# Row gathers and gate scatters in turn on GpSimd's queue, in a decoder step with product-key experts

## The reference

```
def peer_chunk(h, w_q, sub_keys, u_tab, v_tab):
    q = (h @ w_q).reshape(C, PEER_HEADS, 2, D_KEY // 2)
    s = jnp.einsum('cphd,phkd->cphk', q, sub_keys).astype(jnp.float32)
    s1, i1 = lax.top_k(s[:, :, 0], PEER_TOPK)
    s2, i2 = lax.top_k(s[:, :, 1], PEER_TOPK)
    ...
    top_s, top_i = lax.top_k(cand, PEER_TOPK)
    e = jnp.take_along_axis(cidx, top_i, axis=-1)
    g = jax.nn.softmax(top_s, axis=-1)
    a = jax.nn.gelu(jnp.einsum('cpkd,cd->cpk', u_tab[e], h)).astype(jnp.float32)
    return jnp.einsum('cpk,cpkd->cd', (g * a).astype(v_tab.dtype), v_tab[e])
```

## Time and profile before

| | us |
|---|---|
| median of 3 runs | 1051.7 |
| lowest and highest | 1051.29, 1053.26 |
| the profiled execution, its own time | 1053.38 |
| its span (first to last instruction) | 1051.7 |
| TensorE busy | 1023.4 |
| VectorE busy | 806.2 |
| ScalarE busy | 534.9 |
| GpSimd busy | 360.9 |

### The profile page before, as it was taken

One profiled execution on the slowest core, in us unless ns is written; L12 is line 12 of the kernel. 1 busy time (PEld: TensorE's weight loads), 2 busy tenths in 40 slices (PEclk: granted clock), 3 DMA queues, 4 the chain that ended last, 5 costly groups with the idle time before them and its releaser, 6 DMA issues.

```text
span 1051.7 us, 22444 instructions
## 1 busy us (share of the span) xinstructions
PE 1023.4 (97%) x6977; PEld 919.5 (87%) x6977; DVE 806.2 (77%) x1778; ACT 534.9 (51%) x995; POOL 360.9 (34%) x288
## 2 busy tenths in 40 slices
PE   7999999999999999999999999999999999999997
PEld 7997746999999998999999999988878888888875
DVE  4334276686889997895677589979888888888888
ACT  5435565454545444444344645555555555555553
POOL 0244500000057778878888781011011010100100
PEclk9999997999999999999999999999999999999999
DMA  7655997343478879999999967878888888888872
GB/s 271 261 212 171 351 296 233 120 153 129 169 212 232 233 207 273 309 246 273 342 347 358 294 172 237 318 276 296 301 305 296 287 286 294 282 297 284 290 262 96
DMA packets 132346, 270.05 MB, mean 257 GB/s; under 512 B 30112, under 2 KB 79296, under 8 KB 130480
## 3 DMA queue, kind: packets, MB, share of 16 engines
q1 hardware_dynamic: 98352, 205.23, 57.3%
q0 software_dynamic: 33952, 64.33, 21.7%
HBM read 240.99 MB, written 30.57 MB: 258 GB/s over the span
## 4 chain that ended last, share of the span: by engine, by line
PE 41%; POOL 15%; DMA 7%; issue 5%; DVE 3%; ACT 1%; SPq 0%; DVEq 0%; ACTq 0%; POOLq 0%
POOL gates L548 14%; PE ps L1094 10%; PE ps L1095 10%; PE ps L1096 10%; DMA activations<-u_out 4%; PE ps L1071 3%; PE ps L604 3%; PE ps L605 3%; PE ps L606 3%; POOL urow L556 1%; DMA gates<-spread_out,spread_at 1%; DMA a_in<-activations 1%; DVE w_lo L1501 1%; DMA urow<-in_u_rows_dram,expert 1%; DVE w_lo_last L1501 0%
## 5 line engine op out<-in xcount | busy, mean ns | idle before, releaser
L1501 DVE TENSOR_TENSOR w_lo<-ring,w_hi 128x512 fp32r<-128x512 f32 (+1 forms) x439 | 386.3, 885 | 119.2 <-ACT w_hi L1151 100.0
L1151 ACT CAST w_hi<-ring 128x512 fp32r<-128x512 f32 (+1 forms) x437 | 338.0, 774 | 77.9 <-PE ps L1096 58.2
L604 PE MATMUL ps<-h_hi,w_hi 128*128 128x256 f32 (+1 forms) x1128 | 325.1, 288 | 6.7 <-DVE w_lo L1501 4.8
L605 PE MATMUL ps<-h_lo,w_hi 128*128 128x256 f32 (+1 forms) x1128 | 321.6, 285 | 0.0
L606 PE MATMUL ps<-h_hi,w_lo 128*128 128x256 f32 (+1 forms) x1128 | 319.8, 283 | 0.0
L548 POOL DMA_INDIRECT gates<-spread_out,spread_at x128 | 229.7, 1795 | 134.8 <-DVE spread_out L1934 82.5
L604 PEld LDWEIGHTS ps<-h_hi,w_hi 128*128 128x128 f32 x1128 | 215.3, 191 | 8.9 <-DVE w_lo L1501 4.6
L605 PEld LDWEIGHTS ps<-h_lo,w_hi 128*128 128x128 f32 x1128 | 214.5, 190 | 0.0
L606 PEld LDWEIGHTS ps<-h_hi,w_lo 128*128 128x128 f32 x1128 | 212.6, 188 | 0.0
L1094 PE MATMUL ps<-w_hi,y_hi 128*128 128x512 f32 x496 | 193.9, 391 | 0.8 <-DVE y_lo L2026 0.5
L1096 PE MATMUL ps<-w_lo,y_hi 128*128 128x512 f32 x496 | 193.0, 389 | 0.0
(11 more groups left out here) (385 smaller groups left out, 1251.6 us busy)
## 6 DMA issues: line engine op xcount, KB each, us to landing
ring<-in_uT_dram SPq DMA_DIRECT2D x128, 512.0 KB
ring<-in_v_dram SPq DMA_DIRECT2D x128, 512.0 KB
activations<-u_out SPq DMA_DIRECT2D x128, 128.0 KB
a_in<-activations SPq DMA_DIRECT2D x124, 128.0 KB, 4.6
ring<-in_w_in_dram SPq DMA_DIRECT2D x22, 512.0 KB
gates<-spread_out SPq DMA_DIRECT2D x8, 1024.0 KB, 9.6
ring<-in_w_q_dram SPq DMA_DIRECT2D x16, 512.0 KB
gates<-gates POOLq DMA_DIRECT2D x8, 1024.0 KB, 6.9
```

Source lines behind the costliest of these rows:

```text
L604: mm(out, hi, hi_, start=start, stop=False)
L605: mm(out, hi, lo_, start=False, stop=False)
L1151: nc.scalar.copy(w_hi[slot][:, x], ring[:, ring_slot, x]).then_inc(part_hi, 2 if half is None else 1)
L1501: V.tensor_tensor(w_lo[slot][:, x], ring[:, ring_slot, x], w_hi[slot][:, x].bitcast(F32), ALU.subtract).then_inc(part_lo[ring_slot], 2 if ...
```

## The change

The helper `rows_in`, which issued four gathers in a row, becomes `rows_between`, which issues one gather and then one or two scatters. For gathers 0 to 7 two scatters follow each, numbers 48 to 63, and for gathers 8 to 31 one follows each, numbers 80 to 103. Scatters 64 to 79 stay between the two. All waits stay as they were written; no instruction is added or removed.

```diff
-            def rows_in(first):
-                for k in range(first, first + 4):
+            def rows_between(rows, first, each):
+                for k in rows:
                     if k >= 4:
                         pool.wait_ge(u_dot, k - 3)
                     nc.gpsimd.indirect_dma_start(urow[:, k % 4, :], None, u_rows, at_slot(k)).then_inc(ug_in[k % 4], 16)
+                    gates_out(first + each * (k - rows[0]), first + each * (k - rows[0] + 1))
...
             pool.wait_ge(ix_ready, 1)
-            rows_in(0)
-            gates_out(48, 56)
-            rows_in(4)
-            gates_out(56, 64)
+            rows_between(range(8), 48, 2)
             pool.wait_ge(spread_ready, 2)
             gates_out(64, 80)
-            for first in range(8, SLOTS, 4):
-                rows_in(first)
-                gates_out(72 + first, 76 + first)
+            rows_between(range(8, SLOTS), 80, 1)
```

## The result

| | changed, us | before, us | ratio, 95% interval |
|---|---|---|---|
| first comparison | 1069.47 (1066.23 to 1075.24, 4 runs) | 1051.49 (1048.69 to 1053.26) | 1.0148 [1.0104, 1.0193] |
| again, below as `after_again` | 1061.04 (1057.49 to 1067.54, 12 runs) | 1054.18 | 1.0077 [1.0044, 1.0110] |

The change costs 16 to 18 us by the first comparison and 7 to 8 by the second, the longer one. The forecast was +10. Single executions of the kernel before spread from 1046.95 to 1061.43 us in that second set, so few runs place a median only roughly. A difference in us beside a ratio is worked out from that ratio; the medians' own differences are up to 1.7 us away from it, and 2.4 in the first comparison. The profiled execution of the changed kernel was the longest of its four, 1075.24 us, and is read here with `after_again` beside it (1057.49 us).

What follows compares the result with a forecast made beforehand. TensorE, busy 97% of the span, was taken to bound the kernel, losing time only in pauses or at half clock. 12.3 lost minus 2.3 returned gave +10.0 us, median 1061.7 us, range 1054.5 to 1069 for 8 in 10.

Steps and rivals of the forecast that it cites:

- rival A: Rows 8 to 31: VectorE stays row-bound to the end, longer turns or landings pass on whole; +17 us, 1069; chance 0.14.
- GpSimd's turns and the wait at scatter 48: GpSimd at gathers 0 to 3: turns of 5.7 us, scatter 48 waiting until scatter 47 has landed.
- Products 5.7 us apart, each with a wait: VectorE at rows 1 to 3: dots at 415.3, 421.0 and 426.7, each waiting for its DMA.
- the fixed 6.5 us from issue to product: Gathers 1 to 3: each dot taken to start 6.5 us after its gather's issue, between 5.23 and 7.61 seen.
- the 420 that was named as a sign of being wrong: VectorE at row 3: the prediction is wrong if dot 3 starts before 420 us.
- Loss of 12.3 us from rows 0 to 3: TensorE at the first gathers: late rows make w_lo late, costing 12.3 us, bounds 9.1 to 14.0.
- Rows 4 to 7 free: Gathers 4 to 7: landed by 450 us, before VectorE reaches dot 4 at about 470, so no cost.
- A return of 2.3 us from rows 8 to 31: Rows 8 to 31: 2 to 2.5 of 3.9 us idle returned; bounds all 3.9 returned or 5 lost.
- part 3: The prediction's part on rows 8 to 31, one gather and one scatter in turn: a small return, 2.3 us.
- B: Rows 0 to 3: cheap start, landing 5.2 us and no second clock drop; +4 us, 1055.7; chance 0.14.
- C: Faster: waits at dots 8 and 12 go, dots 1 to 3 cost nothing; −3.9 us, 1047.8; chance 0.05.
- D: No change: the stall at rows 0 to 3 is paid back in full; 1052 us; chance 0.07.

Runs made afterwards that it cites:

- early_only: Against the kernel before: only gathers 0 to 7 take turns with two scatters each, gathers 8 to 31 stay in bunches of four; 1056.76 us against 1053.81, ratio 1.0013.
- before_again: The kernel before, unchanged, measured and profiled a second time against itself; ratio 1.0000 [0.9965, 1.0034].
- late_only: Against the kernel before: only gathers 8 to 31 take turns with one scatter each, gathers 0 to 7 stay in bunches of four; 1059.66 us, ratio 1.0069.
- sooner_v_rows_ahead: Kernel before with gathers 0 to 3 and 8 to 31 eight scatters sooner, last three gates loads behind first v gathers; 1050.61 us against 1055.49, ratio 0.9951.
- after_two_lows: Changed kernel with VectorE making two w_lo ahead of dot 0 and one more behind each of dots 0 to 3; 1048.51 us against 1054.18 before.

## Why the prediction came true, step by step

- **Sign, time and range.** Forecast 1061.7 within 1054.5 to 1069: the repeat gave 1061.0, the first comparison 1069.5, half a us above the edge (its ratio on the median of 1051.7 gives 1067.3, inside). The sign was reasoned. That the size came out is luck in good part: the forecast added 12.3 for the early part and −2.3 for the late one, and measured alone they are +1.4 and +7.3. And the 1061.0 stands on a before of 1054.2, so the loss there is 7 to 8 us, not 10; by the first comparison, 16 to 18, rival A's +17 would have been the nearest.
- **GpSimd's turns and the wait at scatter 48: right.** 5.5 to 6.4 us a turn against 5.7, and the wait for landing is exposed where forecast.
- **Products 5.7 us apart, each with a wait: wrong in form.** They came in pairs, over 13.15 us in place of 17.7. In `early_only` they came singly over 18.68 us, near the forecast. The failed term is the fixed 6.5 us from issue to product: it was 8.97 and 4.86 for rows 0 and 1, and 7.90 and 4.73 for rows 2 and 3 (from 405.53, 411.93, 417.46 and 422.92 to the products above). Product 3 started at 427.65, behind the 420 that was named as a sign of being wrong; in the repeat it started at 417.92, but there gather 0 was issued 6.1 us sooner than in the earlier trace rows. By the Trainium skill, "DMA: Bandwidth & Descriptors", the section on the anatomy of one DMA, the estimate was 3.2 us behind the issue. The second row of each pair, issued in 0.99 us, landed at most 3.9 and 3.7 behind it, close to the page; rows 0 and 2, 7.6 and 6.5 behind theirs, are not.
- **Loss of 12.3 us from rows 0 to 3: mechanism right, size too large.** 9.0, 9.5 and 9.0 us in three profiles against the first profile of before, 10.5 to 11.0 against `before_again`, in place of 12.3; my lower bound was 9.1. By the table of the first stretch it is 4.8 us more idling, and 3.5 of clock (0.97 to 0.90 over 50 us), where the forecast had 9.1 of idling and 3.2 of clock. So the idling was sized too large. A single drop of the clock was sized too small: I took 1.6 us for a pause, and the tile at 427.8 took 2.6 more than at full clock. The pauses were two of 3.71 and 3.64 us here, and in the repeat three of 3.51, 2.89 and 2.46, against the forecast's 2.57, 1.9, 2.8 and 4.4.
- **Rows 4 to 7 free: right.** Products 4 to 7 ran from 482.3 to 489 us, in the repeat from 470.7 to 478, and PE has no pause there.
- **A return of 2.3 us from rows 8 to 31: wrong, and it is the step that failed.** `late_only` costs 7.3 us. I had priced the exposed waits at 1.5 to 3 us each and let them vanish in a return; they were 2.82 and 3.14 us, in the repeat 0.30 and 3.13. The wait at scatter 64, which I had not counted, was 6.12 us for 3.41 before, and 4.14 in the repeat, as in `before_again`. Nor had I counted that the last gather of each four now has three more scatters ahead of it. As I took rate and need to be equal (3.7 us a row), nothing was there to absorb them. That was rival A's argument, and part 3 goes its way by half. The wait before product 8 did shrink, from 7.68 to 4.78 us, but the waits for rows were 14, of 32.7 us in all, for 8 of 18.0 us before. The repeats are closer to each other, 27.7 us in 17 for 28.3 in 11, so the total of the waits says less than their number:

```profile
499.67 1.23 DVE L1967 CUSTOM_DVE_ANT_0 urow<-urow,hrow 128x1024 f32<-128x1024 f32 x1 [4.78 <-DMA urow<-in_u_rows_dram,expert]
504.47 1.23 DVE L1967 CUSTOM_DVE_ANT_0 urow<-urow,hrow 128x1024 f32<-128x1024 f32 x1 [2.43 <-DMA urow<-in_u_rows_dram,expert]
509.57 1.22 DVE L1967 CUSTOM_DVE_ANT_0 urow<-urow,hrow 128x1024 f32<-128x1024 f32 x1 [2.73 <-DMA urow<-in_u_rows_dram,expert]
```

- **What the step lacked.** I had the return mechanism (VectorE comes later to product 8), and credited it to the turns. It belongs to the early delay: the second stage gets shorter by it with late bunches (4.7 and 5.9 us) and with late turns (4.0 and 9.1). The late turns themselves only cost. Early alone I put at 12.3 before the result; it measured +1.4 [−2.2, +5.1].
- **My own test**, that the prediction is wrong if PE loses more than 6 us behind 450: it lost 8.24 in the first profile and 4.00 in the repeat. By that test its part 3 falls, though the total stood.
- **Rivals.** A held in part, as said. B's claim that the clock does not drop again is refuted (0.50 at 427.8). C and D are refuted by both intervals; but the early part alone comes near to D's return in full, by its median; by its stages about half of the 9.0 us comes back. **Nothing downstream:** the gates' chain cost nothing in the changed kernel (`y_hi` to end 364.0). Its last gates load went out at 697.83 and the next gather waited 21.43 us for `sacc`.
- **Open:** why the first comparison gives twice the loss of the second. The second stage (156.1 and 151.0) and the third (84.0 and 81.4) make 7.7 us between the two profiles, nearly the gap, but two profiles don't settle it.

## What to carry to other kernels

When a consumer's queue holds tiles for the busiest engine behind waits for gathered rows, ask at each wait how many tiles are in stock, not how long the wait is: here two tiles ahead and one more behind each product removed every pause from 400 to 550 us, with most of the waits still there. A delay early in such a queue is partly repaid later if the later rows have landed by then, and a gain early is charged later if they haven't, so cost both ends of a reordering together, and test its parts apart. Spreading transfers evenly puts more work ahead of the last of each bunch and takes away the cover of waits that stood behind a bunch; here, where rate and need were equal (3.7 us a row), more rows were awaited and it lost.

## What the runs showed of the hardware

- A gather of 512 KB took between 4.73 and 8.97 us from the start of its issue to its product in one chain of four (the two short ones are upper bounds, as their products did not wait), and 5.05, 5.17, 4.29 and 5.64 us in `early_only`. An average of these is not a term that can be added four times.
- Between 400 and 600 us, pauses of PE of 1.62 to 1.75 us left the granted clock high, in five profiles. Pauses of 1.98 and 2.07 us were followed by half clock (`late_only` at 490, the changed kernel at 512), as were the longer ones, with two exceptions: behind 2.16 us in `sooner_v_rows_ahead` and 2.54 us in `after_two_lows` it stayed at 1.00, and these rows don't say why. The table by stretches behind the second:

```profile
581.00:585.00 4.00, 3.44 (x27) 3.26 (x28) 2.95 (x5) 3.69 (x6) 3.42 (x2) 1.00 0.87 265
```

- The part ahead of tile 40 took 393.5 to 407.1 us in fourteen profiles, a spread that is more than most effects of this study, and its length went with the granted clock there (1.00 to 0.96).
- Putting PE's idle time at zero over 200 us gave 0.46% at the end. The time of one stage is no forecast of the span until the start of the next stage is read too.
